# A two-block transformer kernel: the group norm of its recurrent branch cut in three, corrections on other PSUM banks, and another weave

## The reference, cut to what matters

```
def step(S, inp):                       # one token, per head: S is 64 x 64
    sa = einsum('bhvk,bhk->bhv', S, -kk_t)
    S = S * w_t + sa[..., None] * (kk_t * a_t) + v_t[..., None] * k_t
    return S, einsum('bhvk,bhk->bhv', S, r_t)
...
y = (y - mean) * rsqrt(var + GN_EPS)    # over the 64 features of a head
y = y * gn_gain + gn_bias
y = y + sum(r * k * r_k, axis=-1, keepdims=True) * v
y_a = (y * silu(z)) @ w_out_a
...
merged = sigmoid(gate_a) * y_a + sigmoid(gate_b) * y_b
h = h + rmsnorm(merged @ w_o, g_post)
```

## Time and profile before

| | us |
|---|---|
| median of 3 runs | 1569.41 (1569.32 to 1571.57) |
| the profiled execution | 1577.92 |
| its span, first to last instruction | 1576.6 |
| mean granted TensorE clock, as a share of 2.4 GHz | 0.947 |
| TensorE busy | 1425.8 (90%) |
| VectorE, ScalarE, GpSimd busy | 541.3, 350.7, 270.5 |

### The profile page before, as it was taken

How to read it: one execution, slowest core, us unless ns; L and a number is a source line. 1 busy time by engine, 2 the same in 40 slices (tenths; PEclk the granted TensorE clock), 3 DMA queues, 4 the chain that set the end, 5 groups by cost and what they waited for, 6 DMA issues and landing times. The chain is left out here.

```text
span 1576.6 us, 23493 instructions
## 1 busy us (share of the span) xinstructions
PE 1425.8 (90%) x9996; PEld 762.2 (48%) x9996; DVE 541.3 (34%) x1293; ACT 350.7 (22%) x827; POOL 270.5 (17%) x307
## 2 busy tenths in 40 slices
PE   7998998988999996999999949999998898888898
PEld 5544544655444444444444424457775444555443
DVE  3124322556111624411211124343388452232213
ACT  2214323543101111011111113443212111122121
POOL 3010301020440441122222132012230021011000
PEclk9899999998999997999999969989999999898989
DMA  5153012040030358699999871101221243000311
GB/s 190 54 200 134 1 54 82 3 161 2 3 122 39 107 188 306 209 388 375 382 384 384 315 256 67 39 23 54 108 77 30 81 114 115 2 2 15 110 52 53
DMA packets 99323, 208.15 MB, mean 132 GB/s; under 512 B 14725, under 2 KB 22736, under 8 KB 99088
## 3 DMA queue, kind: packets, MB, share of 16 engines
q1 hardware_dynamic: 87152, 171.38, 30.3%
q0 software_dynamic: 12064, 35.22, 6.7%
HBM read 186.12 MB, written 19.42 MB: 130 GB/s over the span
## 5 line engine op out<-in xcount | busy, mean ns | idle before, releaser
L456 PE MATMUL pb<-Wt,HT 128*128 128x512 f32 (+1 forms) x384 | 162.9, 586 | 2.0 <-DVEq L386 2.0
L3305 PE MATMUL pb<-Wt,HT 128*128 128x512 f32 x256 | 123.0, 623 | 4.4 <-DVE AR L3396 4.4
L456 PEld LDWEIGHTS pb<-Wt,HT 128*128 128x128 f32 x384 | 75.0, 216 | 78.6 <-issue 76.3
L456 PE MATMUL pb<-Wt,AR 128*128 128x512 f32 x256 | 111.5, 592 | 0.0
L1889 PE MATMUL pb<-AR 128*64 128x512 f32 x256 | 86.2, 606 | 0.0
L666 PE MATMUL pb<-AR 64*128 64x512 f32 (+7 forms) x256 | 65.2, 499 | 15.5 <-ACT AR L761 4.5
L456 PEld LDWEIGHTS pb<-Wt,AR 128*128 128x128 f32 x256 | 48.1, 190 | 57.9 <-issue 57.9
L3305 PEld LDWEIGHTS pb<-Wt,HT 128*128 128x128 f32 x256 | 47.9, 196 | 57.4 <-issue 49.9
L1889 PE MATMUL pb<-Wt,AR 128*64 128x512 f32 x192 | 70.8, 595 | 0.0
L3317 PE MATMUL pb<-Wt,AR 128*128 128x512 f32 x128 | 67.4, 668 | 1.4 <-ACT AR L793 1.4
L1348 PE MATMUL pb<-Wt,HT 128*128 128x512 f32 x144 | 64.7, 606 | 2.8 <-DVEq L386 2.8
(11 more groups left out here) (530 smaller groups left out, 2350.9 us busy)
## 6 DMA issues: line engine op xcount, KB each, us to landing
Wt<-in_w_in_dram SPq DMA_DIRECT2D x18, 2048.0 KB, 8.4
AR<-in_w_gate_dram SPq DMA_DIRECT2D x8, 2048.0 KB, 18.7
AR<-in_w_up_dram SPq DMA_DIRECT2D x8, 2048.0 KB, 19.1
AR<-in_w_down_dram SPq DMA_DIRECT2D x8, 2048.0 KB, 19.3
Wt<-in_w_gate_dram SPq DMA_DIRECT2D x6, 2048.0 KB, 18.2
Wt<-in_w_down_dram SPq DMA_DIRECT2D x6, 2048.0 KB, 14.3
Wt<-in_w_up_dram SPq DMA_DIRECT2D x6, 2048.0 KB, 21.3
ys<-AR POOLq DMA_DIRECT2D x1, 5632.0 KB, 21.2
```

Of the source, the lines that this page charges most:

```text
L456: r = mm(s[:, 0:n], lT[:, k, t * 128:(t + 1) * 128], w[:, k, c0:c0 + n], start=k == 0, stop=k == nk - 1)
L3305: r = mm(s, HT[:, k, t * 128:(t + 1) * 128], W.ap(("gate2", c, br))[:, k, :], start=k == 0, stop=k == 7)
```

## The change

The diff, cut to what the prediction speaks of. `rstd_ve` is only cut in two, so that its end can stand elsewhere.

```diff
@@ apply(n), VectorE, features
                 ve.wait_ge(s_rk, n + 1)
-                if n < 3:
-                    ve.wait_ge(s_dia, n + 1)
                 ve.wait_ge(s_exp, n + 1)
@@
-        rows_of = [(1, 10), (10, 14), (14, 17), (17, 19), (19, 21), (21, 23)] + [(t, t + 1) for t in range(23, 32)]
-        lead_steps, load_steps, store_steps = 4, 2, 4
+        rows_of = [(1, 9), (9, 12), (12, 14), (14, 16), (16, 18), (18, 20)] + [(t, t + 1) for t in range(20, 32)]
+        lead_steps, load_steps, store_steps, norm_steps = 1, 3, 5, 3
@@ chunks_pe
+            def corrections(t, group):
+
+                s = {i: P.take(pe, "T", ("m", t, i)) for i in group}
...
                 r.then_inc(P.full(("akv", t)), 1)
+                if t > 0:
+                    ended[t - 1] = True
                 yield 1
...
-                s = P.take(pe, "T", ("q", t))
+                s = P.take(pe, "S", ("q", t))
...
-                for group in ((0, 1, 2), (3,)):
-                    s = {i: P.take(pe, "T", ("m", t, i)) for i in group}
...
+                corrections(t, (0, 1, 2))
                 yield 1
...
-                    if i == 0 and t < 3:
+                    if i == 0:
+                        corrections(t, (3,))
+                    if i == 1 and t < 3:
                         own(t, (3,))
-                ended[t] = True
-                yield 1
+            for _ in range(norm_steps):
+                yield 1
+            ended[3] = True
+            yield 1
@@ chunks_ac, tile t
                 yield 1
+                if t > 0:
+                    group_square_ac(t - 1)
                 yield 1
...
+                if t > 0:
+                    group_root_ac()
+                    ended[t - 1] = True
                 yield 1
@@ chunks_ve, tile t
             for t in ALLT:
+                if t > 0:
+                    group_mean_ve(t - 1)
                 yield 1
...
-                yield 1
+                if t > 0:
+                    group_square_ve(t - 1)
+                yield 1
+                if t > 0:
+                    group_norm_ve(t - 1)
+                    ended[t - 1] = True
                 yield 1
...
+                for i in range(3):
+                    correction(i)
                 ve.wait_ge(s_pre, 5 * t + 1)
                 ve.wait_ge(*P.filled(("q", t)))
...
+                correction(3)
@@ tensor_second, scalar_second, vector_second
-            weave(dense_pe(ended), chunks_pe(ended), 3, 4)
+            weave(dense_pe(ended), chunks_pe(ended), 4, 5)
```

More of the change, by code:

```diff
@@ L3025, in own @@
                                 r.then_inc(P.full(("r", 0)), 1)
+            def corrections(t, group):
+                s = {i: P.take(pe, "T", ("m", t, i)) for i in group}
+                for n, hp in heads2:
+                    for i in group:
+                        q, h = slice(32 * i, 32 * i + 32), 2 * n + hp
+                        r = mm(s[i][64 * hp:64 * hp + 64, 64 * n:64 * n + 64], Zt[q, h, 0:64],
+                               beTM[q, 64 * h:64 * h + 64], start=True, stop=True)
+                        if (n, hp) == (3, 1):
+                            r.then_inc(P.full(("m", t, i)), 1)
             for t in ALLT:
@@ L3229, in chunks_ac, with group_mean_ve, group_square_ve, group_norm_ve @@
                     yield 1
[L3230 to L3234, removed]
-                yield 1
+            yield 1
+            group_square_ac(3)
+            yield 1
+            group_root_ac()
+            yield 1
+            ended[3] = True
+            yield 1
+        def group_mean_ve(t):
+            y = v8(YB)
+            for hp in range(2):
+                ve.wait_ge(*P.drained(("y", t, hp)))
+            ve.chain(lambda: vt.reduce_sum(mu8, y, AX.X))
+            ve.chain(lambda: vt.tensor_scalar(mu8, mu8, 1.0 / 64, None, ALU.mult))
+            ve.after()
+            vt.tensor_tensor(y, y, bc(mu8, 64), ALU.subtract).then_inc(s_yc, 1)
+        def group_square_ve(t):
+            ve.wait_ge(*square_h.nxt())
+            ve.chain(lambda: vt.reduce_sum(va8, v8(YQ), AX.X))
+            ve.after()
+            vt.tensor_scalar(m8, va8, 1.0 / 64, GN_EPS, ALU.mult, ALU.add).then_inc(s_mean, 1)
+            ve.chain(lambda: vt.tensor_tensor(v8(YQ), v8(vTM[:, t, :]), bc(dia[:, t, :], 64), ALU.mult))
+        def group_norm_ve(t):
+            y = v8(YB)
+            rstd_end_ve(rs8c, m8, y8)
+            ve.wait_ge(s_gn, 32)
+            ve.chain(lambda: vt.tensor_tensor(y, y, bc(rs8c, 64), ALU.mult))
+            ve.chain(lambda: vt.tensor_tensor(YB, YB, gnb[:, 0:512], ALU.mult))
+            ve.chain(lambda: vt.tensor_tensor(YB, YB, gnb[:, 512:1024], ALU.add))
+            ve.chain(lambda: vt.tensor_tensor(YB, YB, YQ, ALU.add))
+            ve.wait_ge(s_za, 1)
+            ve.after()
+            vt.tensor_tensor(oA[:, t, :], oA[:, t, :], YB, ALU.mult).then_inc(s_out2, 1)
         def chunks_ve(ended):
@@ L3264, in chunks_ve, with correction @@
                 yield 1
+                def correction(i):
+                    ve.wait_ge(s_pre, 5 * t + 2 + i)
+                    ve.wait_ge(*P.filled(("m", t, i)))
+                    vt.tensor_tensor(Mt[:, i], P.ap(("m", t, i))[:, 0:256].rearrange("p (n k) -> p n k", k=64),
+                                     Mt[:, i], ALU.add).then_inc(P.free(("m", t, i)), 1)
+                for i in range(3):
+                    correction(i)
                 ve.wait_ge(s_pre, 5 * t + 1)
@@ L3621, in scalar_second @@
             ended = {}
-            weave(dense_ac(ended), chunks_ac(ended), 3, 4)
+            weave(dense_ac(ended), chunks_ac(ended), 4, 5)
             last_ac()
@@ L3630, in vector_second @@
             ended = {}
-            weave(dense_ve(ended), chunks_ve(ended), 3, 4)
+            weave(dense_ve(ended), chunks_ve(ended), 4, 5)
             last_ve()
```

53 lines of the change are left out of this document (19 added, 34 removed).

## The result

The changed kernel takes **1527.2 us** (median of 4 runs, 1524.46 to 1532.97), the kernel before 1570.5 on the same chip (4 runs, 1569.32 to 1575.07). The ratio is 0.972, 95% interval 0.969 to 0.976: 43.3 us faster, where the forecast was 36 (1533, range 1525 to 1550). The profiled execution took 1526.49 us with a span of 1525.2; before it was 1577.92 and 1576.6.

The account below looks back on a forecast made before the run. TensorE, busy 90% of the span, bounds the kernel, with waits and slow clock costing 63 us. Terms −5.6 + 3.4 − 0.3 − 9.4 − 19.8 − 7.6 = −39.3, less 3 reserve, −36: 1569.4 to 1533 us; range 1525 to 1550.

Parts of the forecast that it names:

- More: Rival: the slow-clock pieces left in corrections, turns and tail (5.1 us) and the 3 us held back vanish; 1525 or below; chance 0.06.
- reserve: 3 us taken back from the summed gain, as in-order streams cannot be followed to a tenth and several places are tight.
- features: Feature products: without VectorE's wait on the row sums, TensorE's 3.95 us wait and a 1.7 us slow piece go; −5.6 us.
- start of the chunks: Turns of v with one lead step: new 3.2 us wait behind the Silu plus one slow piece, less 1.5; net +3.4.
- inverses: First inverse rows: TensorE waits 2.6 us for the second gate's add, where it waited 2.9 before; −0.3 us.
- corrections and boundaries: Two forecast terms together: corrections on other banks (−9.4 us) and waits and slow clock at tile boundaries (−19.8 us).
- tail: Behind the last chunk step: sixteen gate matmuls cover tile 3's group norm; −4.6 idle and −3.0 clock, −7.6 us.
- Corrections: With q on ring S, TensorE's waits at the corrections go: −6.0 us idle, −3.4 us of slow clock.
- Boundaries: Tile boundaries: dividing the group norm removes 12.0 us of TensorE waits and 8.3 of slow clock, 0.3 new twice; −19.8 us.
- P: End of source line L3134 in a tile, from which the prediction counted its boundary times in us.
- slower: Rival: the divided norm ends behind the corrections and delays the chain; norm would end at P + 29; 1573 or more; chance 0.05.
- half of it: Rival: boundary waits come back at z and the corrections, three tiles losing 14 us together; 1547, range 1543 to 1557; chance 0.18.

Follow-up runs that it names:

- experiment 1: Changed kernel with the wait of VectorE's apply(n) on the row sums put back for n below 3: 1532.8 us, 0.977 of the kernel before.
- experiment 7: Changed kernel with ScalarE's Silu of the first gates moved from the features' end to behind the copies of the block products: 1524.3 us, ratio 0.971.
- experiment 3: Changed kernel with q back on a bank of ring T and its add ahead of the first three corrections' adds on VectorE: 1529.1 us, ratio 0.974.
- experiment 4: Changed kernel with the group norm of tiles 0 to 2 in one piece again on VectorE and ScalarE, TensorE's program untouched: 1543.2 us, ratio 0.982.
- experiment 5: Changed kernel with the old weave, three chunk steps in four dense steps instead of four in five: 1563.0 us, ratio 0.997.
- experiment 6: Changed kernel with four lead steps in place of one: 1549.3 us, ratio 0.988.
- experiment 9: Changed kernel with both the group norm of tiles 0 to 2 whole and the old weave of three in four: 1552.2 us, ratio 0.986.
- experiment 10: Kernel before with only the change's numbers: weave four in five, lead, load and store steps 1, 3, 5, new inverse rows: 1566.7 us, ratio 0.995.
- experiment 8: Changed kernel with four lead steps and two store steps in place of one and five: 1526.4 us, ratio 0.969.
- experiment 11: Changed kernel with two lead steps and four store steps in place of one and five: 1525.7 us, ratio 0.970.
- experiment 12: Experiment 8's kernel with the own terms of chain steps 0 to 2 issued one dense step later: 1519.9 us, ratio 0.967.

## Why the prediction was right, step by step

The time, 1527.2, lay in the forecast's own range (1525 to 1543), near its lower end. Of what the rival "More" named, the slow pieces in the corrections and the tail and the 3 us of reserve were indeed not there; the one at the turns came, and a second with it. Term by term, in us of the stretch:

| term | forecast | measured | how |
|---|---|---|---|
| features | −5.6 | −5.7 | their end, 36.91 to 31.21; experiment 1: 6.3 |
| start of the chunks | +3.4 | +3.8 | the two timelines |
| inverses | −0.3 | −1.8 | wait for the gate's add 2.86 to 1.11 |
| corrections and boundaries | −29.2 | −31.7 | what is left of 44.75 |
| tail | −7.6 | −9.4 | last chunk step to w_o, less 12.0 of gates |
| sum | −39.3 | −44.8 | |
| reserve | +3 | 0 | |

**Features, start.** As forecast, down to the new wait: 3.07 us at L2728 for 3.2, and two slow pieces for one.

```profile
1206.15 1.94 PE L2728 MATMUL pb<-cst,AR 128*128 128x128 f32 x8 [3.07 <-ACT AR L3195]
1207.88 3.62 PE L3357 MATMUL pb<-Wt,HT 128*128 128x512 f32 x4
```

The number was right and the reason half right: the prediction named the Silu alone, and experiment 7 shows a second cause that ends with it.

**Corrections.** All 6.0 us of idle time went, as forecast. Of its clock term (3.4) no run shows anything: in experiment 3, where 4.0 us of the waits are back, no slow piece begins behind a correction.

**Boundaries.** Priced 19.8, and 19.4 in experiment 4. That the totals agree so well is partly luck: the waits that the divided norm took away are 9.0 us and not 12.0, since the 4.8 us at and behind the turn of `oA` are not among them, and the clock is 10.4 and not 8.3. The turn waited before in one tile of three, behind tile 2, where only three gate steps (5.4 us) stood between the last chunk step and it; the order of the steps took that away. The places and the room were right: corrections at P + 19.3 (P + 19.5 forecast), norm done at P + 19.5 in tile 0 (P + 18 to 19.4 forecast), no wait at z in tile 3. The two table loads per tile cost no wait; timeline of ScalarE in the changed kernel, the norm of tile 2:

```profile
1411.72 1.28 ACT L406 ACT_TABLE_LOAD   x1
1413.01 0.21 ACT L410 ACTIVATE SM<-SM 128x8 f32<-128x8 f32 x1
```

The next instruction starts 1.29 us after the load. The further drain of 1.38 us that the Trainium skill ("ScalarE: Activation LUTs", What ACT_TABLE_LOAD costs) adds does not show here either; the row decides.

But the divided norm is worth this only where gate steps are left at the boundary (the new weave with its own lead and store steps; experiments 5 and 6 lack them), and that is **the step that was missing**. The prediction had one clause on it, "Up projection: its `oA` is read behind that", and did not work out how far behind. It was 2.4 us in tile 0, and the turn is the first thing to wait when the gates run out. The rival "slower" asked how late the norm would end against the corrections; what makes it slow in experiments 5 and 6 is a turn that comes early, with the norm in its place. The rival "half of it" looked at z and the corrections and not at the turn.

**Weave.** The prediction gave it the tail, 7.6 us, and took the rest as separate. Experiments 5, 6, 9 and 10 show that the terms cannot be added up one at a time: numbers alone −3.7, divided norm +12.4 under the old weave and −19.4 under the new one. As far as I can see the forecast came out since its places (P + so much) were read off the new program as a whole, with the new order of TensorE under every term. The row "corrections and boundaries" above is a remainder and no measurement of its own.

**Tail.** −9.4 for −7.6: the slow piece that I left there did not come. Sixteen gate matmuls in one row, then two short waits, as forecast:

```profile
1435.75 14.00 PE L3357 MATMUL pb<-Wt,HT 128*128 128x512 f32 x32
1449.59 1.47 PE L792 MATMUL pb<-cst,AR 128*128 128x128 f32 x12
1451.77 2.04 PE L792 MATMUL pb<-cst,AR 128*128 128x128 f32 x16 [0.71 <-ACT AR L797]
1454.61 7.13 PE L3369 MATMUL pb<-Wt,AR 128*128 128x512 f32 x16 [0.80 <-ACT AR L797]
```

What lay under the forecast as a whole is the clock: from 1219 to 1522 us there is no slow piece, where I had left two, and the reserve of 3 us was not needed.

## What to carry to other kernels

When a long operation is cut up and moved off one wait, follow its last piece to everyone who reads it, and work out the room of each: here the reader that bound when the order was changed was the turn of `oA`. Where two streams are woven by a ratio, count what is left of the covering work at each boundary, from the first one on, and not the ratio alone: with the norm divided and three or four gate steps left nothing waited, with one TensorE stood 2.9 us and with none 7.7. The ratio (12.5 or 13.3 dense steps against thirteen) says only which way this number drifts, and experiment 6 ran out at 12.5. And a wait that ends for two reasons within 0.1 us does not go with one of them.

## What the runs showed of the chip

**Stops in long rows of small matmuls.** Inside the row of 128 records of L3118 and 96 of `own`, TensorE stopped with nothing awaited in most tiles, mostly for 0.8 to 1.7 us, and for 3.2, 3.4 and 4.1 us in tile 0 of experiments 9, 5 and 6; in the row of 256 of the block products for 2.0 to 2.6 us. The stop has a fixed place: in the changed kernel and in experiments 1, 3, 4, 7, 8 and 11 it comes behind record 81, 75 and 43 of `own` in tiles 0, 1 and 2, and in tile 3 the same row ran through. In experiment 12, with two larger matmuls of 0.9 us each put between, the stops of tiles 0 and 1 were gone; with a turn of 0.7 us between, that of tile 2 fell from 1.4 to 0.7 us. So longer work put into the row takes the stop away, in one execution each. That the row's length alone makes it is not shown: the edit also moved the records in the program, and the unbroken row of tile 3 never stopped. That it is the supply of instructions is a guess.

**The clock is not a function of the code.** Behind the same wait of 3.07 us at the turns of v, the next gate matmuls took 3.62 us in the changed kernel and 1.88 in experiment 3:

```profile
1205.30 1.11 PE L2728 MATMUL pb<-cst,AR 128*128 128x128 f32 x8 [3.07 <-ACT AR L3195]
1206.24 1.88 PE L3357 MATMUL pb<-Wt,HT 128*128 128x512 f32 x4
```

Seven profiled executions have this wait of 3.07 us. The two gate matmuls behind it took 3.62 us in three of them (the changed kernel, 4 and 9), 2.90 and 2.51 in experiments 1 and 10, and 1.88 in 3 and 5. A slow piece behind one wait is therefore a chance and not a price, up to 1.7 us when it comes. Where the waits at a boundary were longer or followed each other, as in experiments 4, 5 and 10, slow pieces came at every boundary of tiles 0 to 2.
